# Recurrence stage: products grouped by row height, gate pieces moved, decay exponentials one part per level

## What is computed

```python
def rwkv_scan(r, w, k, v, kk, b, s0, reverse):
    def step(s, inp):
        r_t, w_t, k_t, v_t, kk_t, b_t = inp
        sa = jnp.einsum('bhvk,bhk->bhv', s, kk_t)
        s = s * w_t[:, :, None, :] - sa[..., None] * b_t[:, :, None, :] + v_t[..., None] * k_t[:, :, None, :]
        return s, jnp.einsum('bhvk,bhk->bhv', s, r_t)
    ...
def merge_branches(y_a, y_b, y_c, zg, p):
    y = jnp.stack([y_a, y_b, y_c], axis=2)
    gates = jax.nn.sigmoid(zg.astype(F32)).reshape(zg.shape[:2] + (3, D_MODEL))
    merged = jnp.sum(jnp.einsum('btnc,ncd->btnd', y, p['w_branch']) * gates, axis=2)
    return merged @ p['w_out']
```

## Time and profile before

| | us |
|---|---|
| median of 3 runs | 2528.96 (2528.1 to 2529.77) |
| the profiled execution, its own time | 2519.51 |
| its span, first to last instruction | 2517.7 |
| TensorE busy in the span | 2066.8 (82%) |
| the recurrence stage, from its first Gram group to its last gate piece | about 743 to 1490 |

### The profile page before, as it was taken

One profiled execution on the slowest core, in us unless ns is written; L12 is line 12 of the kernel. 1 busy time (PEld: TensorE's weight loads), 2 busy tenths in 40 slices (PEclk: granted clock), 3 DMA queues, 4 the chain that ended last, 5 costly groups with the idle time before them and its releaser, 6 DMA issues. The chain is left out here.

```text
span 2517.7 us, 41126 instructions
## 1 busy us (share of the span) xinstructions
PE 2066.8 (82%) x16339; PEld 1575.7 (63%) x16339; DVE 933.0 (37%) x1863; ACT 491.8 (20%) x928; POOL 685.4 (27%) x1030
## 2 busy tenths in 40 slices
PE   7989879979769989999999975975829999999800
PEld 7666545546548777777777765932528888877600
DVE  0734221207624444333454332734251222222267
ACT  0211122112123233232332312100102222212100
POOL 4416000000013233232332211312013444444423
PEclk9989878789989898888998887997769999999955
DMA  7233344545131120211210016600128998999572
GB/s 236 67 117 101 122 138 139 175 173 191 59 115 52 44 73 19 59 57 34 66 40 24 7 49 246 214 33 18 45 73 323 334 322 305 334 341 323 211 308 100
DMA packets 244753, 358.31 MB, mean 142 GB/s; under 512 B 38305, under 2 KB 173236, under 8 KB 240772
## 3 DMA queue, kind: packets, MB, share of 16 engines
q1 hardware_dynamic: 216734, 299.42, 35.2%
q0 software_dynamic: 24560, 45.27, 5.0%
q10 hardware_dynamic: 3318, 11.59, 1.3%
HBM read 308.42 MB, written 85.65 MB: 157 GB/s over the span
## 5 line engine op out<-in xcount | busy, mean ns | idle before, releaser
L440 PE MATMUL ps_s<-hT,w_in_sb 128*128 128x512 f32 x432 | 214.6, 654 | 0.0
L2688 DVE TENSOR_TENSOR me_hh<-me_sg,ps_ju 128x128 f32<-128x128 f32 x76 | 21.9, 288 | 398.8 <-PE ps_jd L2645 375.3
L1262 PE MATMUL ps_gs<-hT,gt_w 128*128 128x512 f32 x256 | 147.6, 660 | 11.0 <-PEq L75 7.3
L440 PEld LDWEIGHTS ps_s<-hT,w_in_sb 128*128 128x128 f32 x432 | 89.9, 214 | 105.1 <-issue 104.9
L2637 PE MATMUL ps_jg<-me_xT,me_wg 128*128 128x128 f32 x1216 | 149.0, 276 | 0.0
L2637 PE MATMUL ps_ju<-me_xT,me_wu 128*128 128x128 f32 x1216 | 148.2, 275 | 0.0
L2645 PE MATMUL ps_jd<-me_wd,me_hh 128*128 128x512 f32 x304 | 143.9, 596 | 2.4 <-DVE me_yb L2694 2.4
L2637 PEld LDWEIGHTS ps_jg<-me_xT,me_wg 128*128 128x128 f32 x1216 | 142.7, 193 | 0.1
L2637 PEld LDWEIGHTS ps_ju<-me_xT,me_wu 128*128 128x128 f32 x1216 | 141.9, 192 | 0.0
L2666 ACT ACTIVATE me_xT<-ps_jx 128x1024 f32<-128x1024 f32 x77 | 78.9, 1024 | 256.7 <-PE ps_jx L2628 256.7
L2628 PEld LDWEIGHTS ps_jx<-ident,me_xg 128*128 128x128 f32 x616 | 79.4, 192 | 72.2 <-DMA me_xg<-h_dram,me_ids 43.1
(11 more groups left out here) (536 smaller groups left out, 4207.3 us busy)
## 6 DMA issues: line engine op xcount, KB each, us to landing
me_wg<-in_exp_w_gate SPq DMA_DIRECT2D x76, 512.0 KB
me_wu<-in_exp_w_up SPq DMA_DIRECT2D x76, 512.0 KB
me_wd<-in_exp_w_down SPq DMA_DIRECT2D x76, 512.0 KB
cb_rows<-yj_dram SPq DMA_DIRECT2D x10, 2048.0 KB
w_ad_sb<-in_w_ada SPq DMA_DIRECT2D x32, 512.0 KB
w_in_sb<-in_w_in SPq DMA_DIRECT2D x31, 512.0 KB
gt_w<-in_w_in SPq DMA_DIRECT2D x24, 512.0 KB, 4.1
zr<-in_w_ada SPq DMA_DIRECT2D x4, 2048.0 KB, 10.6
```

The lines of the kernel that those rows point to most:

```text
L440: mm(ps_s[:, b, :], w_in[:, r, k, :], hT[:, k, 0:TS], start=(k == 0), stop=(k == KT - 1))
L1262: nc.tensor.matmul(ps_s[:], w[:, t % WR, k, :], hT[:, k, 0:TS], start=(k == 0), stop=(k == KT - 1))
```

## The change

Three things change, all inside `rwkv_units`.

1. In the right-hand side and in the output products, all eight state products (64 rows) now stand first and all eight token products (128 rows) behind them.
2. The letters move. GRAM, GA twice and TURNED G become GRAM GA, LAST G ahead of the Gram group k = 4, and TURNED AG around the transposes. STATE and NEXT shrink from GAG to GA each; the two freed G stand at RHS, behind the right-hand side, and at SOLVE, behind the output products and ahead of the solve. A unit still has 12 G and 14 A, and no product is added or removed.
3. `exps` is cut in three, at j = 1, 2 and 3 in place of j = 2.

The gate piece that stood behind k = 4 now stands between k = 3 and k = 4. The diff, cut to its core (the letters on the other engines follow TensorE's):

```diff
-FILL_GRAM, FILL_TURNED, FILL_MID, FILL_LEVEL = "GA", "G", "GA", "A"
-FILL_STATE, FILL_NEXT = "GAG", "GAG"
+FILL_GRAM, FILL_LAST, FILL_TURNED, FILL_MID, FILL_LEVEL = "GA", "G", "AG", "GA", "A"
+FILL_RHS, FILL_SOLVE, FILL_STATE, FILL_NEXT = "G", "G", "GA", "GA"
...
+                        if k == 4:
+                            fill(FILL_LAST)
...
-                    fill(FILL_GRAM)
+                    fill(FILL_TURNED[0])
                     pe.wait_ge(m.c_gd, n * 8 + 6)
...
-                    fill(FILL_TURNED)
+                    fill(FILL_TURNED[1])
...
                             for q in range(MT):
                                 for e in range(2):
-                                    mm(bank[2 + e][:, q, 0:HD], a_[half[e], q, :], sts[half[e], q, :], start=True, stop=False)
+                                    mm(bank[2 + e][:, q, 0:HD], a_[half[e], q, :], sts[half[e], q, :], start=(q == 0), stop=False)
+                            for q in range(MT):
                                 for e in range(2):
-                                    last = mm(bank[2 + e][:, q, 0:HD], akt[:, e, q, :], vh(n, 2 * q + e), start=False, stop=True)
+                                    last = mm(bank[2 + e][:, q, 0:HD], akt[:, e, q, :], vh(n, 2 * q + e), start=False, stop=(q == MT - 1))
                                     if q == MT - 1:
                                         last.then_inc(m.c_rh_mm, 1)
+                            fill(FILL_RHS)
...
                     for q in range(MT):
                         for e in range(2):
                             mm(bank[2 + e][:, q, 0:HD], r_[half[e], q, :], sts[half[e], q, :], start=(q == 0), stop=False)
+                    for q in range(MT):
                         for e in range(2):
                             mm(bank[2 + e][:, q, 0:HD], rkt[:, e, q, :], vh(n, 2 * q + e), start=False, stop=False)
+                    fill(FILL_SOLVE)
                     pe.wait_ge(m.c_yup, (n + 1) * (2 * LJ))
...
-                def exps(n):
+                def exps(n, k):
...
-                        if j == 2 and n + 1 < UNITS:
-                            exps(n + 1)
+                        if 1 <= j <= 3 and n + 1 < UNITS:
+                            exps(n + 1, j - 1)
```

More of the change, by code:

```diff
@@ L1588, in _ @@
                 for n in range(UNITS):
-                    fill(2 * FILL_GRAM + FILL_TURNED + 5 * FILL_MID + 4 * FILL_LEVEL)
+                    fill(FILL_GRAM + FILL_LAST + FILL_TURNED + 5 * FILL_MID + 4 * FILL_LEVEL)
                     if n + 2 < UNITS:
                         load(n + 2)
-                    fill(FILL_LEVEL + FILL_STATE + FILL_NEXT)
+                    fill(FILL_LEVEL + FILL_RHS + FILL_SOLVE + FILL_STATE + FILL_NEXT)
                 fill.rest()
@@ L1776, in _ @@
                         V.tensor_tensor(yi[:, e], yi[:, e], bc4(idc[:]), ALU.add).then_inc(m.c_y1, 1)
-                    fill(FILL_GRAM + FILL_TURNED)
+                    fill(FILL_LAST + FILL_TURNED)
                     dve.wait_ge(m.c_bo_mm, n + 1)
@@ L1812, in _ @@
                             fill(FILL_LEVEL)
-                    fill(FILL_STATE)
+                    fill(FILL_RHS + FILL_SOLVE + FILL_STATE)
                     dve.wait_ge(m.c_s_mm, n + 1)
@@ L1827, in _ @@
                 fill = Lane(t_act(act), g_act(act))
-                def exps(n):
+                def exps(n, k):
                     d, c = n % 2, DECAY_C
[L1832 to L1836, removed]
+                    if k == 0:
+                        act.wait_ge(m.c_d, n + 1)
+                        if n:
+                            act.wait_ge(m.c_stage, n)
+                        A(ex[:, 0], dm[:] if d == 0 else dp[:], ACT.Exp, scale=-c if d == 0 else c)
+                        return
+                    if k == 1:
+                        A(ex[:, 1], dm[:] if d == 0 else dp[:], ACT.Exp, scale=c if d == 0 else -c)
+                        return
                     A(ex[:, 2], dp[:] if d == 0 else dm[:], ACT.Exp, scale=-c if d == 0 else c)
@@ L1844, in squares @@
                     A(yq[:], ys[:], ACT.Square).then_inc(m.c_sq, 1)
-                exps(0)
+                for k in range(3):
+                    exps(0, k)
                 fill(FILL_START)
@@ L1855, in _ @@
                         squares(n - 1)
-                    fill(FILL_GRAM)
+                    fill(FILL_LAST + FILL_TURNED[0])
                     for b, out in ((2, ktok), (3, btok)):
@@ L1937, in _ @@
                         G.tensor_tensor(xi[:, e], xi[:, e], bc4(idc[:]), ALU.add).then_inc(m.c_x1, 1)
-                    fill(2 * FILL_GRAM + FILL_TURNED)
+                    fill(FILL_GRAM + FILL_LAST + FILL_TURNED)
                     for j in range(LJ):
@@ L1952, in _ @@
                             fill(FILL_LEVEL)
-                    fill(FILL_STATE + FILL_NEXT)
+                    fill(FILL_RHS + FILL_SOLVE + FILL_STATE + FILL_NEXT)
                 centre(UNITS - 1)
```

## The result

The changed kernel takes 2446.26 us (median of 4 runs, 2445.43 to 2450.34) against 2528.53 us of the kernel before (4 runs). The ratio is 0.9682, with a 95% interval of 0.9664 to 0.9700. The forecast was 2450 us, 79 us less; measured are 82 us less.

A forecast was written before the change was run, and what follows sets the result against it. The prediction took TensorE to bound the recurrence stage, leaving its running speed and waits to gain from. Its terms, 76 - 4 + 4 + 6 - 3, gave 79 us less, from 2529 to 2450 us, with a range of 2434 to 2484.

The forecast's parts named there:

- Term 1: Ten unit tails: grouped products at full clock take 94 us in place of 170.5, 76 us less.
- allowance of 4 us for leftover falls: In the tails: the clock still falls in one or two units, about 3 us each, 4 us back.
- Term 2: First gate product behind each tail: no longer slow, 4 us less in all.
- Term 3: Ahead of Gram group k = 4: the gate piece at LAST covers ten waits for an eviction, 6 us less.
- Term 4: STATE to NEXT and NEXT to GRAM: attention steps closer together, so more waiting for exponentials, 3 us back.
- The exponentials, costed at nothing: ScalarE at j = 1 to 3: splitting the decay exponentials changes the time by under 1 us either way.
- A: Tails: the clock still falls in every unit after the first block; 48 us less, 2481; chance 14%.
- B: Grouped blocks: no closer spacing, each token record waits for its own load; 34 us less, 2495; chance 4%.
- C: Tails: clock falls as now, and gate pieces at RHS and SOLVE run slow inside the low stretch; 2555; chance 2%.
- D: Shorter tails: exponentials, the solve's copy or the state sum stop TensorE 2 us a unit more; 2470; chance 7%.

The follow-up runs named there:

- halves-apart kernel: The changed kernel with each block's eight state products ordered by half of the partitions in place of alternating halves; 2504.28 us, ratio to before 0.9922.
- e4: The changed kernel with VectorE's preparation of the next unit cut over levels 0 to 2 and all five decay exponentials at level 3; 2428.66 us.
- e8: The kernel before plus grouping, VectorE's preparation cut over levels 0 to 2, exponentials at level 3, letters as before the change; 2429.03 us.

## Why the prediction was right

**Term 1, the tails, 76 less 4.** The tails took 170.5 us and take 127.5 - 5 x 3.54 - 5 x 2.46 = 97.5 without gate pieces, 73.0 less where 72 was forecast. Each part of the sum came out: the block 2.87 (2.9), the products like L1644 1.07, the solve's rest 1.54 from 797.09 to 798.63 (1.4). The allowance of 4 us for leftover falls came out in part by luck: one tail of ten, 994.42 to 1009.51, with a wait of 0.78 us shortly ahead of it, is 3.2 us longer than its like, but in the second profiled execution no tail lost the clock.

**But the reason given for the clock was half wrong.** The forecast named "a denser block, a gate piece" in one breath and put the return of the clock down to the pieces. The runs part them: without pieces the clock holds in ten tails of ten, and with pieces but alternating blocks it holds in one. The forecast had about 20 us for height and the rest for clock. Measured are 17 and 56, but both come from the one edit, since the closer spacing is also what keeps the clock. The number would have been the same for a kernel without any new letter, and the forecast didn't see that. Nor do the levels keep full clock throughout, as it said: in the kernel before five low stretches lie in them, 20 us together, behind waits of 1.7 to 4.0 us.

**Term 2, behind the tail, 4.** Right: the first gate product behind the tail has 1.12 us as at full clock, where it had 1.29 and 1.84. The clock record was low for 7.3 us in all behind the ten tails, which is worth 3.6 us, and is not low there any more.

**Term 3, the wait ahead of k = 4, 6.** This step failed. The waits went, as forecast, but "what is late next" was answered with the evictions of VectorE alone. ScalarE's copy of the transposes came late in its place (3.0 us), and more time at the low clock took the rest; undoing it costs nothing.

**Term 4, attention, 3 back.** 25.6 us in 22 waits became 25.9 in 23. The 3 us didn't come in these waits. There are 2.0 us of waits for ScalarE's copy of a Gram group (L1863) instead, in the profiles with the new letters and in none without them. The exponentials, costed at nothing, were worth nothing that shows.

**The sum.** The stage lost 77.3 us: 73.0 in the tails, 3.6 behind them and 4.8 in waits (TensorE's idle stretches of over 0.15 us add up to 47.8 before and 43.0 after), less 2.0 because the rest of the stage is at the low clock for 30.5 us where it was for 26.4. That makes 79.4; the 2 us left over are not placed. So the total of 79 has term 1 right and is helped by terms 3 and 4, whose errors cancel: together they were to give 3 us, and the waits less the clock gave 2.8.

**The rivals.** A fell with the clock line of the tails. B fell with L1661, sixteen token records in 1.83 us, 114 ns apart, while each load takes 192 ns; in the halves-apart kernel records of one half start 112 ns apart while their loads take 188. So by these records the rule of the Trainium skill (TensorE: Matmul & The Clock Gate, The mechanism), that loads overlap products in flight only when row groups differ, doesn't hold for these float32 products (the same section excepts loads into a background weight buffer, which no run here can tell apart). Alternating row groups is still worth something, 0.49 us a block, since such products run side by side. C, given 2%, was not the result, but slow pieces inside the low stretch are what the letters meet without the grouping. D fell with TensorE's idle time, which is 4.8 us less and not 20 more.

## What to carry to other kernels

Read the distance between starts, not busy time: a stretch that shows TensorE 100% busy took a third more time for alternating heights (3.82 us against 2.87) and then lost half of its clock. Group small products by the rows that they use and, within a height, alternate the halves; and do it for all blocks of a sparse stretch, since here one sparse block ahead took the gain of a dense one behind it. When two edits of a change aim at the same low clock, run each alone before believing in either.

## What the runs showed of the hardware

- A change between 64 and 128 rows costs about 0.14 us at full clock. A block with eight of them, the one behind it counted, takes 3.82 us. One with a single change, which has a gate piece of 128 rows behind it, takes 2.87, so 0.95 for seven.
- In the tails TensorE was 100% busy in every kernel, and the granted clock held or fell with how closely the small products stood. In the eight profiled executions whose first block was grouped with alternating halves (2.87 us, or 2.97 without a gate piece behind it), 78 of 80 first blocks kept 2.4 GHz. With first blocks of 3.4 us (halves apart) the clock fell in or at the start of the first block in nine units of ten. With blocks of 3.8 us it did so in nine of ten with the new letters; in the kernel before it fell in the first block of five units and within 2 us behind it in the other five.
- Once the clock was low, a grouped block (5.5 us at half) didn't bring it back in any of ten units, though the same block kept a clock that was full.
- A wait that goes away can be paid back in clock: 3.6 us fewer in waits and 10 us more at the low clock gave the same stage. e4 and e8 show the same trade, 6 us against 10. The reason was not tried.
